# Expert sums as 64 by 64 products on TensorE, and who adds the first eight rows of tile 0

## What is computed

```
h = rmsnorm(x + mixer(x))
for each of 8 heads: 16 experts per token are picked (two top-16 lists, 16 best sums)
act = gelu(sum_d h[d] * peer_down[expert][d])          # the dot of a token with its expert row
out = sum over 128 picks of  gate * act * peer_up[expert]   # the weighted sum of expert rows
y = rmsnorm(x + mixer(x) + out)
```

## Time and profile before

| what | value |
|---|---|
| time, median of 3 runs | 1668.24 us (1667.35 to 1669.12) |
| span of the profiled execution | 1665.7 us, 2.5 us below the median |
| PE busy | 1393.7 us, 84% |
| DVE busy | 1176.3 us, 71% |
| ACT, POOL busy | 573.7 us (34%), 704.4 us (42%) |
| read from HBM | 604.19 MB, of it gathers 570.46 MB |

### The profile page before, as it was taken

One profiled execution on the slowest core, in us unless ns is written; L12 is line 12 of the kernel. 1 busy time (PEld: TensorE's weight loads), 2 busy tenths in 40 slices (PEclk: granted clock), 3 DMA queues, 4 the chain that ended last, 5 costly groups with the idle time before them and its releaser, 6 DMA issues.

```text
span 1665.7 us, 15170 instructions
## 1 busy us (share of the span) xinstructions
PE 1393.7 (84%) x4311; PEld 684.3 (41%) x4311; DVE 1176.3 (71%) x2555; ACT 573.7 (34%) x1785; POOL 704.4 (42%) x633
## 2 busy tenths in 40 slices
PE   7999999897897889779977897799779977777743
PEld 6744465553453345334433443344334433333311
DVE  3997858966776777677666776777777777677755
ACT  2212231532333333333333333333333343333342
POOL 0004624544454444354444454444444444444452
PEclk9999999999999889998999999999999999999965
DMA  7203227999999999999999999999999999999996
GB/s 292 102 1 94 115 85 284 379 421 421 422 421 421 422 421 421 421 421 421 421 422 422 421 421 421 422 420 421 420 413 421 420 413 420 421 414 414 411 412 256
DMA packets 87987, 608.46 MB, mean 365 GB/s; under 512 B 11104, under 2 KB 13664, under 8 KB 16224
## 3 DMA queue, kind: packets, MB, share of 16 engines
q0 software_dynamic: 78336, 570.46, 82.8%
q1 hardware_dynamic: 9568, 37.04, 6.0%
HBM read 604.19 MB, written 2.88 MB: 364 GB/s over the span
## 4 chain that ended last, share of the span: by engine, by line
PE 42%; DMA 36%; DVE 13%; issue 4%; POOL 2%; ACT 2%; DVEq 1%; ACTq 0%; POOLq 0%; SPq 0%
DMA arena<-experts,expert 36%; PE ps L1668 23%; PE ps L1531 8%; DVE arena L1311 5%; PE ps L1631 5%; PE ps L1511 4%; POOL arena L599 2%; DVE cst L1288 1%; DVE cst L1291 1%; DVE picked L1294 1%; PE ps L1490 1%; PE ps L1602 1%; ACT late L907 1%; PE ps L1528 1%; DVE best_i L1249 1%
## 5 line engine op out<-in xcount | busy, mean ns | idle before, releaser
L1668 PE MATMUL ps<-arena,late 128*128 128x512 f32 x2016 | 961.2, 630 | 198.6 <-ACT late L907 198.2
L599 POOL DMA_INDIRECT arena<-experts,expert x544 | 632.2, 1162 | 748.6 <-PE ps L1668 648.5
L1311 DVE CUSTOM_DVE_ANT_0 arena<-arena,hn 128x1024 f32<-128x1024 f32 x544 | 655.5, 1223 | 363.2 <-DMA arena<-experts,expert 351.4
L1668 PEld LDWEIGHTS ps<-arena,late 128*128 128x128 f32 x2016 | 393.6, 201 | 742.3 <-issue 457.0
L893 ACT ACTIVATE gl<-dots 128x2 f32<-128x2 f32 (+1 forms) x274 | 55.9, 204 | 793.6 <-DVE dots L1311 789.8
L907 ACT ACTIVATE late<-cst,weight 128x128 f32<-128x128 f32 (+1 forms) x536 | 183.7, 390 | 18.9 <-issue 0.3
L896 ACT ACTIVATE weight<-gl,gate 128x1 f32<-128x1 f32 x544 | 131.0, 287 | 19.4 <-issue 0.7
L1531 PE MATMUL ps<-arena,hT 128*128 128x512 f32 x256 | 111.1, 593 | 0.0
L1631 PE MATMUL ps<-hT,region_b 128*128 128x272 f32 x448 | 106.9, 392 | 0.0
L1631 PEld LDWEIGHTS ps<-hT,region_b 128*128 128x128 f32 x448 | 85.1, 190 | 27.9 <-issue 12.4
L1062 DVE SCALAR_TENSOR_TENSOR region_b<-region_b,par 128x574 f32<-128x574 f32 x120 | 92.6, 814 | 4.5
(11 more groups left out here) (174 smaller groups left out, 873.9 us busy)
## 6 DMA issues: line engine op xcount, KB each, us to landing
arena<-weights SPq DMA_DIRECT2D x6, 2048.0 KB, 11.2
region_b<-head_weights SPq DMA_DIRECT2D x8, 1152.0 KB
arena<-experts,expert POOLq DMA_INDIRECT x544
hT<-x_turned SPq DMA_DIRECT2D x2, 1088.0 KB, 7.7
arena<-weights SPq DMA_DIRECT2D x4, 512.0 KB, 11.1
xs<-x_prompt SPq DMA_DIRECT2D x4, 512.0 KB, 9.9
arena<-weights SPq DMA_DIRECT2D x2, 1024.0 KB, 14.2
y_prompt<-xs SPq DMA_DIRECT2D x4, 512.0 KB, 3.8
```

The costliest lines, as they stand in the source:

```text
L599: pool.indirect_dma_start(rows_of(n), None, experts, bass.IndirectOffsetOnAxis(ap=expert[:, vt % BUFS, k:k + 1], axis=0))\
L1311: last = v.tensor_tensor_reduce(out=rows_of(n)[:, 0:D], in0=rows_of(n)[:, 0:D], in1=hn[:, tile_of(vt)], scale=1.0, scalar=0.0, op0=ALU.mul ...
L1668: last = mm(ps[:, 2 * (vt % 2) + half, :], diag[:, n % DIAGS, :], rows_of(n)[:, D + half * SEC:D + (half + 1) * SEC], start=k == first * G ...
```

## The change

TensorE's sums are written as four products of a 64 by 64 piece of the diagonal each (token half `i`, column half `half`) where there were two products of the whole diagonal. A piece takes its tokens from 64 partitions and writes to the 64 partitions of PSUM that `half` names, in the bank that `i` names; so in a bank there lie now the 64 tokens of half `i`, columns 0 to 511 on partitions 0 to 63 and columns 512 to 1023 on partitions 64 to 127. DVE's `add` becomes four adds of 64 x 512 instead of one of 128 x 1024.

`sum_here` is gone, and with it the early end of ACT's `step` for these rows. The first eight rows of tile 0 go through ACT's diagonals and TensorE like all others: `("sum", 0, 0)` stands behind `query(1)`, `("sum", 0, 1)` behind `ret_out(4)`. With the first sum the point moves up from which TensorE's steps have four banks instead of eight.

```diff
-HERE = 2
+TOKENS = P // 2
@@ plan()
-    order += mix(2, 0) + turn("ffn_t", 1) + out(3) + head(4) + mix(2, 1) + query(1) + back(3) + scores(4) + keys(1)
-    order += mix(3, 0) + [("ret_out", 4)] + mix(3, 1) + [("ret_state", 4)] + back(4) + mix(4, 0) + mix(4, 1)
+    order += mix(2, 0) + turn("ffn_t", 1) + out(3) + head(4) + mix(2, 1) + query(1) + sums(0, 0) + back(3) + scores(4) + keys(1)
+    order += mix(3, 0) + [("ret_out", 4)] + sums(0, 1) + mix(3, 1) + [("ret_state", 4)] + back(4) + mix(4, 0) + mix(4, 1)
@@ step()
-                if vt == 0 and g < HERE:
-                    return
@@ VectorE's list
-            sum_here(0)
-            sum_here(1)
@@ add()
-                total = ps[:, 2 * (vt % 2):2 * (vt % 2) + 2, :].rearrange("p b n -> p (b n)")
-                v.tensor_tensor(out=xs[:, tile], in0=total, in1=xs[:, tile], op=ALU.add).then_inc(s_acc, 1)
+                for i, half in product(range(2), range(2)):
+                    total = ps[half * TOKENS:(half + 1) * TOKENS, 2 * (vt % 2) + i, :]
+                    part = xs[i * TOKENS:(i + 1) * TOKENS, tile, half * SEC:(half + 1) * SEC]
+                    last = v.tensor_tensor(out=part, in0=total, in1=part, op=ALU.add)
+                last.then_inc(s_acc, 1)
@@ sum_up()
-                    for half in range(2):
-                        last = mm(ps[:, 2 * (vt % 2) + half, :], diag[:, n % DIAGS, :],
-                                  rows_of(n)[:, D + half * SEC:D + (half + 1) * SEC], start=k == first * GROUP,
+                    for i, half in product(range(2), range(2)):
+                        tokens = slice(i * TOKENS, (i + 1) * TOKENS)
+                        last = mm(ps[half * TOKENS:(half + 1) * TOKENS, 2 * (vt % 2) + i, :],
+                                  diag[tokens, n % DIAGS, tokens],
+                                  rows_of(n)[tokens, D + half * SEC:D + (half + 1) * SEC], start=k == 0,
                                   stop=k == TOPK - 1)
```

More of the change, by code:

```diff
@@ L2 @@
 from contextlib import ExitStack
+from itertools import product
 import numpy as np
@@ L895, in step @@
                 for k in rows:
-                    ready = nc.scalar.activation(weight[:, vt % 2, k:k + 1], gl[:, vt % 2, k:k + 1], ACT.Copy,
+                    nc.scalar.activation(weight[:, vt % 2, k:k + 1], gl[:, vt % 2, k:k + 1], ACT.Copy,
                                                  scale=gate[:, vt % BUFS, k:k + 1])
-                    if vt == 0 and g < HERE:
-                        ready.then_inc(s_diag, 1)
-                if vt == 0 and g < HERE:
-                    return
                 act.drain()
@@ L1315, in weigh @@
                         last.then_inc(s_dot, 1)
-            def sum_here(g):
-                for k in range(g * GROUP, (g + 1) * GROUP):
-                    dve.wait_ge(s_diag, k + 1)
-                    v.scalar_tensor_tensor(out=xs[:, 0], in0=rows_of(k)[:, D:2 * D], scalar=weight[:, 0, k:k + 1],
-                                           in1=xs[:, 0], op0=ALU.mult, op1=ALU.add).then_inc(s_used, 1)
-                    dve.drain()
             def add(vt):
@@ L1648, in sum_up @@
             def sum_up(vt, g):
-                first = 0 if vt else HERE
-                if g == first and vt >= 2:
+                if g == 0 and vt >= 2:
                     pe.wait_ge(s_acc, vt - 1)
-                elif g == first:
-                    if vt == 0:
-                        pe.wait_ge(s_used, HERE * GROUP)
+                elif g == 0:
                     for before in BEFORE_SUMS[2 * vt:2 * vt + 2]:
```

## The result

The changed kernel takes 1676.18 us (median of 4 runs, 1675.14 to 1677.25), the kernel before, beside it, 1667.80 (4 runs, 1666.67 to 1669.12). The ratio is 1.0046 with a 95% interval of 1.0033 to 1.0058: **slower by 8.4 us** by the medians, 7.7 by the ratio. The forecast was 1676.1 in a range of 1671.0 to 1683.0. The profiled execution after is the longest of the four, 1677.25 us with a span of 1675.5; the span before was 1665.7, so the two traces are 9.8 us apart.

A forecast was written before the change was run, and what follows sets the result against it. Gathers bound the kernel behind 310 us, so only DMA idle time in the opening counts: 8.3 + 1.1 - 1.5 = 7.9 us on 1668.2 (span 1665.7 plus 2.5) gives 1676.1 us, range 1671.0 to 1683.0.

The forecast's parts named there:

- What bounds: Behind 310 us the gathers set the pace, 2.49 us a row; only DMA idle time before that counts.
- A row on TensorE, 0.88 us: PE's sums: four 64 by 64 pieces run side by side, so a row takes 0.88 us instead of 1.76.
- rivals 2 and 3: Pieces two at a time: 1.76 us a row, 1679.9 us, chance 0.09; none side by side: over 2050, chance 0.02.
- Removed from DVE, and added to ACT, 0: Opening: DVE loses some 11 us of sums, ACT gains eight diagonals of 0.39 us; each worth 0.
- Rows 0 to 3, +8.3: Opening: these sums wait behind PE's query, row 6 is issued at 272.0 instead of 263.76; DMA pause grows 8.3 us.
- Rows 4 to 7, +1.1 at row 11: Opening: their later sums issue row 11 at 287.9 against 278.54, 1.1 us more DMA idle.
- Given back, -1.5: Between 280.8 and 310 us: a fuller DMA queue closes most of the 5% idle time, -1.5 us.
- Rows 8 and on, 0: `ffn_t(2)` waits about 2 us for a bank, row 20 is 7.5 us later, less than the queue's lag: 0.
- Behind 310 us, 0: PE saves 436 us on 496 rows and slots come back earlier, into an already full queue: 0.
- The fourth rival, the clock: PE at 1.2 GHz for long stretches; queries in seven heads cost 5 us each: 1711 us, chance 0.03.
- The signs: Right: row 6 near 272, pause some 17 us. Wrong: row 6 before 268, late rate above 415 GB/s, last dot under 4 later.
- the first rival: Late stretch, 1150 to 1650 us: quicker sums win back 4.5 us of DMA waiting, 1670.3 us, chance 0.09.

The follow-up runs named there:

- kernel 1: Kernel before with the 64 by 64 products behind row 8 and four adds; DVE still sums rows 0 to 7: 1668.42 us, ratio 0.9997.
- kernel 3: Changed kernel with the sums of rows 0 to 3 put ahead of the projection and the query: 1676.01 us, ratio 1.0048.
- kernel 4: Kernel before with the gathers of rows 6 to 9 held until PE's `ret_yT(3)`, nothing else added: 1674.06 us, ratio 1.0035.
- kernel 5: Kernel before with some 3.6 us of repeated PE products at each of the two places of the moved sums: 1675.12 us, ratio 1.0040.
- kernel 6: Changed kernel with rows 0 to 3 summed ahead of `mix(2, 1)` and rows 4 to 7 ahead of `mix(3, 0)`: 1677.33 us, ratio 1.0052.
- kernel 7: Changed kernel with DVE's `ret_state(4)` two adds earlier, so `ffn_t(2)` finds its bank read: 1676.06 us, ratio 1.0039.
- kernel 8: Kernel before with DVE's sums of rows 0 to 3 and POOL's gathers of rows 6 to 9 put earlier: 1668.77 us, ratio 1.000.
- kernel 9: Kernel before with the 64 by 64 products behind row 8, and all that frees rows 6 to 23 moved up on four engines: 1675.59 us, ratio 1.0041.

## Why the prediction was right, step by step

- **What bounds.** Right, and shown: the rate of the gathers sets the pace behind 310 us (kernel 1), and the lag of the opening is carried to the end (the table).
- **A row on TensorE, 0.88 us.** 3.66 / 4 = 0.915 us. Against the 7.03 / 16 x 8 = 3.5 us of the pieces one after another that is 3.8-fold. Two at a time and none side by side (rivals 2 and 3) are refuted. The Trainium skill ("TensorE: Matmul & The Clock Gate", Part 3) gives 3.07-fold for four pieces that split the rows, by which a row was estimated at 1.15 us; this is another way of cutting the array, and here the measurement decides.
- **Removed from DVE, and added to ACT, 0.** Right for the first: PE had no gap in which to profit. The diagonals of rows 0 to 3 were not waited for: PE goes from the query (268.49 + 3.73) to the sums at 272.16 without a gap.
- **Rows 0 to 3, +8.3.** The issue of row 6 was 9.8 us later, 8.5 without the shift of 1.3, so the gate was sized rightly: 272.0 forecast, 272.3 when shifted. The pause grew by only 7.6, since packets came 1.9 us after the issue (273.56 to 275.50) instead of the 2.8 that I carried over; POOL took 1.09 us over that issue instead of 2.12.
- **Rows 4 to 7, +1.1 at row 11.** Row 11 was to go out at 287.9, and did at 287.5 when shifted. The extra idle time did not come: the stretch behind the pause is 14.2 us at .91 in both kernels.
- **Given back, -1.5.** Did not come. **This is the step that failed in its reason**: I held the 5% of idle time up to 310 us for a fixed amount that a fuller queue would close. But row 15 waits for `ret_yT(4)`, row 16 for `mix_out(4, 0)`, both behind the sums on PE, so the gaps moved along with the lag: .95 over 29.7 us against .95 over 29.2. Within that stretch something was given back and lost again: counted from row 0, the DMA had moved 2.9 MB less than before at 290 us, 2.3 MB less at 298 and 3.4 MB less at 310, with rows 15 and 16 late in between. Terms of +1.1 and -1.5 that both came out near 0, and a pause 0.7 shorter, cancel to 7.6 + 0.5 = 8.1 where 7.9 was forecast. Part of the closeness to 1676.1 is luck.
- **What the sum did not see.** It ascribed the loss to row 6. Kernels 3 to 6 show two causes side by side, each enough by itself for most of it: a row 6 that is late (5.9 us alone), and 7.3 us of PE work ahead of `ret_yT(4)` (6.7 alone). They do not add, since both end in a row 15 that is late by nearly the same (counted from row 0, 6.2 us in kernel 4, 7.0 in kernel 5, 7.4 in the change), and with either one taken away at least 5.9 of the 8.4 us stay.
- **Rows 8 and on, 0.** Right. The bank wait came, 2.92 us for the 2 forecast, and the query behind it took 5.74 us instead of the 3.84 of kernel 7. Row 20 was 8.9 us late, counted from row 0, where 7.5 were forecast; the queue had work all the same (a DMA share of 1.01 from 308 to 326 us).
- **Behind 310 us, 0.** Right. PE's sums fell by 293 us, not by the 436 of the forecast: a row costs 668.3 / 512 = 1.31 us over the whole run, against 0.915 in the opening. PE works less there, and the granted clock is .82 and .75 where it was .95 and .89. The fourth rival, the clock, was right in that the clock falls and wrong in its price: no slice of the page between 330 us and the last one shows less than 414 GB/s. The Trainium skill (same page, Part 1) says that the throttled clock is the idle state and that activity releases it. The trace agrees in direction: less work, less clock. The queries of the later heads, by which that rival was priced, took 403 ns a record over the run against the 392 of the earlier trace rows (L1621, 448 records, 111.4 us), so they hardly slowed.
- **The signs.** Row 6 near 272, a pause of 17 us (16.9), 3.7 us for four rows (3.66) and a last dot as late as the kernel were right. The sign "a rate above 415 GB/s would prove me wrong" was a bad one: it is 418, and the forecast held. Part of the 411 of the earlier trace rows was the end of the run, which now falls behind 1650 us; the rest is below.
- **Slips in the working, none of weight.** The eighth slice of the earlier trace rows is at 379 GB/s; 421 holds from the ninth on. In the first rival 500 x 10 / 421 is 11.9 us and not 11. What lies around the span is 1.75 us in the profiled execution after (1677.25 against 1675.5); the 2.5 us of the table before are that and the distance of its profiled execution from the median.

## What to carry to other kernels

When a queue is full for three quarters of a kernel, look for the moment at which it fills for good, and judge every change by how much later that moment comes; work that was made cheaper behind it was worth nothing here, however much. Before moving work from an engine with slack to one without a gap, list the gates that lie behind it on that engine's list in order of time: a single gate moved up only handed its pause to the next (kernels 3 and 8), and two causes of lateness cost far less together than their sum (5.9 and 6.7 us alone, 8.4 together). Making moved work cheaper (here 2 x 3.66 us instead of 2 x 7) bought back about the time by which the last of those gates came earlier: 6.0 us, with row 15 6.4 us earlier.

## What was not expected of the hardware

**One DMA engine ends alone.** At the end the mean rate is no measure of the pace. Busy time by stretch of the kernel before, columns as in the earlier trace rows:

```profile
1644.00:1648.00 4.00, 1.35 (x16) 0.24 (x8) 1.91 (x4) 0.70 (x4) 0.00 (x0) 0.50 0.10 41
1648.00:1652.00 4.00, 3.02 (x24) 0.80 (x24) 3.53 (x6) 1.34 (x5) 0.00 (x0) 0.50 0.07 29
1652.00:1655.00 3.00, 1.08 (x8) 0.20 (x8) 2.97 (x6) 1.19 (x5) 0.00 (x0) 0.50 0.06 27
```

and of the change:

```profile
1654.00:1658.00 4.00, 1.28 (x13) 0.20 (x4) 1.69 (x4) 0.91 (x4) 0.00 (x0) 0.50 0.07 29
1658.00:1662.00 4.00, 3.02 (x24) 0.80 (x24) 3.74 (x6) 1.25 (x6) 0.00 (x0) 0.50 0.06 27
1662.00:1665.00 3.00, 1.08 (x8) 0.20 (x8) 2.97 (x4) 1.22 (x6) 0.00 (x0) 0.50 0.06 25
```

A share of .06 is one sixteenth, and 25 to 29 GB/s is one sixteenth of 421 (26): for the last 7 to 11 us one of the 16 engines works and the other 15 are done. The dots of these last rows still start 2.4 to 2.6 us apart (before at 1645.89, 1648.47, 1650.83, 1653.29 and 1655.75), as they did with all engines at work (2.49). That fits a row being there only when its last engine is through, with the slowest engine setting the pace all along and a higher mean rate meaning only that the others run further ahead of it; the profile does not name the engines, so this is argued and not shown. It fits the 3 GB/s of kernel 1 that brought no time; why one engine is slower, none of these runs shows. The nine rows that the prediction saw waiting at the end were then partly rows waiting for that one engine.

**A PE that had stood came back at half its clock.** In four of these kernels PE stood for a step of DVE, and the granted clock behind the gap was .50, that is 1.2 GHz. In kernel 4 it stood 2.83 us, the clock was .50 from 285 to 291 us, and the projection took 9.94 us instead of 7.13. In the change it stood 2.92 us, the clock was .50 from 307 to 313, and the query took 5.74 us instead of 3.84. In kernel 7 it stood 3.06 us, the clock was .50 from 314 to 320, and four rows took 5.72 us instead of 3.66. In kernel 9 it stood 3.84 us, and the projection took 9.62 us; the stretch behind it:

```profile
276.00:284.00 8.00, 8.00 (x20) 3.10 (x20) 6.94 (x14) 0.86 (x5) 5.63 (x5) 0.50 0.88 291
```

The kernel before was granted 1.00 up to 310 us. Not every gap did this: behind one of 2.36 us in kernel 3 the query took 3.84 us. In these four a gap on PE in the opening cost more than itself.

**POOL was slow beside DVE's dots.** The same five steps of POOL took 6.7 us in kernel 9, while DVE made dots, and 2.9 us in kernel 8, while DVE stood. That the dots are the reason is argued from the order of the two kernels and not tested alone; kernel 9's row 10 hung on it.
